# The weight differences of a seven-product block, made by GpSimd and not by VectorE

## The chip, the cores and the metric

The kernel runs on one core of a Trainium2 chip. The metric is the device time of one launch in microseconds (us). The kernel before takes 1770.96 us, the median of 3 runs (1770.84 to 1770.96).

## The reference

The reference is a chain of two transformer blocks over 512 tokens of width 1024, in fp32. The first block has windowed and block-sparse attention, the second consists of two layers with other mixers. What matters here are the three MLPs (`m0` in the first block, `m1` and `m2` in the second):

```python
y = jnp.square(jax.nn.relu(h @ w_in)) @ w_out     # w_in 1024x4096, w_out 4096x1024
x = x + y                                          # gated in m0
```

Everything else (norms, projections, attention, scans, convolution) is as before in both kernels and is not touched by the change.

## The kernel before, in words

**Precision.** Every fp32 weight of 128x1024 ("a chunk") is split in two parts before TensorE uses it. ScalarE copies the chunk, rounded, to `WH` (line 1262, `hi`), and VectorE writes the remainder, chunk minus `WH`, to `WL` (line 1852, `lo`, which counts the semaphore `w_lo`). Each product then takes three matmuls: lines 529 to 531 in `three`, and lines 855 to 857 in `product`. `WH` and `WL` have three slots (`NHL`), so `hi` of chunk n waits until TensorE is done with chunk n-3, and TensorE starts on chunk n after it has worked through n-2 and n-1.

**MLP blocks.** Each MLP is worked in four blocks of 1024 hidden features. Ten of the twelve are in the list `FAST`: (m0, 1), (m0, 2), and all four of m1 and of m2. Such a block first runs eight chunks of `w_in` (one 128x512 result each, evicted by ScalarE at line 1468 as relu and at 1470 as square; VectorE then makes differences of quarters of the hidden activations at lines 2161 to 2177 and remainders at line 2150). Then it multiplies by its 1024x1024 part of `w_out` in the way of Winograd and Strassen: seven products of quarters in place of eight (`PRODUCTS`, in the order `ORDER`). Each product has two weight chunks, c = 0 and c = 1, so a block has fourteen of them, called here half 0 to half 13: B11 (halves 0 and 1), B21 (2, 3), T2 (4, 5), T1 (6, 7), T3 (8, 9), B22 (10, 11), T4 (12, 13).

**The weight differences.** The T's are not loaded but made, by eight instructions a block (`t_add`, lines 2087 to 2106), each a subtraction of two 128x1024 fp32 tiles in SBUF: T1 = B12 - B11, T2 = B22 - T1, T3 = T2 - B11, T4 = B21 - T2, for c = 0 and c = 1. They are done in place: in `BP` (four tiles of `ARENA`) and in `TX` (one is `CSB`, the other is the last slot of `RAW`). Each waits for its loads (`park0` to `park5`) or for earlier differences (`tadd`). T3 c also waits until half c has its remainder, since it overwrites B11, and T4 c until half 4+c has its remainder, since it overwrites T2. Their readers are `hi` and `lo` of halves 4 to 9, 12 and 13. SP, which issues all weight loads, waits on `tadd` where a B21 tile in `RAW` is to be overwritten.

**Order on VectorE.** `fast_block` writes the order out: T1 of c = 0 behind input chunk 2, T1 (c = 1) and T2 (c = 0) behind chunk 4, T2 (c = 1) behind chunk 6, T3 behind steps 1 and 3 of the loop over the halves, T4 behind steps 5 and 7. Step s of that loop (1 to 13) first does the `lo` of half s+2, so that its last two steps are for chunks of what follows; the `lo` of halves 0 to 2 stand between the input chunks 5 to 7. In between, `y_read` adds finished products from PSUM (lines 2112 and 2116).

**GpSimd** has nothing to do in these blocks. Its program (line 2683 on) is 35 DMA issues and a few memsets. It waits from 309 to 702 us for the end of m0, and from 705 to 1227 us for the end of m1.

Of the kernel before, what the change touches and what calls it, by code (L numbers as in the profile page):

```python
# [13 lines left out]
ALU = mybir.AluOpType  # L14
# [29 lines left out]
FAST = (("m0", 1), ("m0", 2), ("m1", 0), ("m1", 1), ("m1", 2), ("m1", 3), ("m2", 0), ("m2", 1), ("m2", 2), ("m2", 3))  # L44
# [118 lines left out]
FB = {f: n for n, f in enumerate(FAST)}  # L163
# [29 lines left out]
def count(tag, i):  # L193

    return 32 * TAGS.index(tag) + i + 1


def count_lo(tag, i):

    return count(tag, i) + 8 * sum(f < (tag, i // 8) for f in FAST)  # L200
# [19 lines left out]
def split_of(tag, blk, p, c):  # L220

    return NO[tag + "p", 14 * blk + 2 * p + c]
# [67 lines left out]
def build(nc, W, X, CV, PAR, CON, OH, BAND, LNG, LNB, SGB, SGW, RB, OUT):  # L290
    scr = nc.dram_tensor("bias_scratch", (16, 640), F32)

    with ExitStack() as ctx:
# [3 lines left out]
        sem = Sems(lambda name: ctx.enter_context(nc.semaphore(name)))  # L297
# [18 lines left out]
        BP = [ARENA[:, 12288 + 1024 * n:13312 + 1024 * n] for n in range(4)]  # L316
        TX = [CSB[:], RAW[:, NRAW - 1, :]]
# [11 lines left out]
        def r32(ap):  # L329
            return ap.bitcast(F32)  # L330
# [70 lines left out]
        T2, acol, emc, cs8 = ar.take(S), ar.take(16), ar.take(16), ar.take(2, 32)  # L401
# [1442 lines left out]
        def vector(e):  # L1844
# [239 lines left out]
                cf, cm = COLS["final"][0], COLS["mix0"][0]  # L2084
                e.tensor_tensor(gs[:, 0:8], par[:, cf:cf + 8], par[:, cm:cm + 8], ALU.mult)

            def t_add(tag, blk, name, c):
                at = FB[tag, blk]
                b11, b12 = BP[c], BP[2 + c]
                if name == "T1":  # L2090
                    e.wait_ge(sem[f"park{c}"], 32 + 16 * (at + 1))
                    e.wait_ge(sem[f"park{2 + c}"], 32 + 16 * (at + 1))
                    e.tensor_tensor(b12, b12, b11, ALU.subtract).then_inc(sem["tadd"])
                elif name == "T2":
                    e.wait_ge(sem[f"park{4 + c}"], 32 + 16 * (at + 1))
                    e.wait_ge(sem["tadd"], 8 * at + 1 + c)
                    e.tensor_tensor(TX[c], TX[c], b12, ALU.subtract).then_inc(sem["tadd"])
                elif name == "T3":
                    e.wait_ge(sem["tadd"], 8 * at + 3 + c)
                    e.wait_ge(sem["w_lo"], split_of(tag, blk, 0, c) + 1)  # L2100
                    e.tensor_tensor(b11, TX[c], b11, ALU.subtract).then_inc(sem["tadd"])
                else:
                    e.wait_ge(sem["tadd"], 8 * at + 5 + c)
                    e.wait_ge(sem["w_lo"], split_of(tag, blk, 2, c) + 1)
                    b21 = raw((tag + "b", 10 * blk + 6 + c))[0]
                    e.tensor_tensor(TX[c], b21, TX[c], ALU.subtract).then_inc(sem["tadd"])

            def y_add(tag, row, col, tt, b, done):

                z, y = part_of(tag, row, col, tt), blocks(ps(b), 4)  # L2110
# [31 lines left out]
            def fast_block(tag, blk, norm):  # L2142
                at, lows = FB[tag, blk], count_lo(tag, 8 * blk) - 1
                adds = (tag, blk - 1) in FAST or tag == "m2"
                x0, x1, x2, x3 = [TMP[:, n, :] for n in range(4)]
                a11, a21, a12, a22 = x0[:, 0:256], x0[:, 256:512], x1[:, 0:256], x1[:, 256:512]

                def h_lo(name, k, m, src):
                    e.wait_ge(sem["mlp_hi"], lows + 4 * k + m)
                    e.tensor_tensor(combo(name, False, k), src, r32(combo(name, True, k)),  # L2150
                                    ALU.subtract).then_inc(sem["mlp_lo"])

                for c in range(8):
                    i, k, did = 8 * blk + c, c // 2, 16 * at + 4 * (c // 2)
                    if c or (tag, blk - 1) in FAST:
                        lo()
                    e.wait_ge(sem["mlp_sq"], count(tag, i))
                    if c % 2 == 0:
                        if blk or k:
                            e.wait_ge(sem["mlp_lo"], lows + 4 * k - 1)  # L2160
                        e.tensor_tensor(x2[:, 0:256], a11, a21, ALU.subtract).then_inc(sem["hs"])
                        h_lo("A11", k, 1, a11)
                        if c == 2:
                            t_add(tag, blk, "T1", 0)
                        elif c == 4:
                            t_add(tag, blk, "T1", 1)
                            t_add(tag, blk, "T2", 0)
                        elif c == 6:
                            t_add(tag, blk, "T2", 1)
                    else:  # L2170
                        e.tensor_tensor(x2[:, 256:512], a21, a22, ALU.add).then_inc(sem["hs"])
                        e.wait_ge(sem["hs"], did + 2)
                        if blk or k:
                            e.wait_ge(sem["mlp_lo"], lows + 4 * k)
                        e.tensor_tensor(x3[:, 0:256], x2[:, 256:512], a11, ALU.subtract).then_inc(sem["hs"])
                        e.wait_ge(sem["hs"], did + 3)
                        e.tensor_tensor(x3[:, 256:512], a12, x3[:, 0:256], ALU.subtract).then_inc(sem["hs"])
                        h_lo("A12A22", k, 2, x1)
                        if c == 7:
                            lo()  # L2180
                        h_lo("S31", k, 3, x2)
                        h_lo("S24", k, 4, x3)
                    if blk == 0 and c == 1:
                        token_mean(tag, norm)
                turned = (tag, blk) in TURNED
                for s in range(1, 14):
                    if turned and s in (10, 12):
                        y_read(tag, blk, ORDER[s // 2 - 1])
                        lo()
                        quarter_sum(tag, s // 2 - 4)  # L2190
                        continue
                    lo()
                    if turned and s == 9:
                        quarter_sum(tag, 0)
                    if s in (1, 3):
                        t_add(tag, blk, "T3", s // 2)
                    elif s in (5, 7):
                        t_add(tag, blk, "T4", s // 2 - 2)
                    elif s == 4 and (tag, blk + 1) not in FAST:
                        kept_read(tag, blk)  # L2200
                    elif s % 2 == 0 and s != 4 and (adds or s > 8):
                        y_read(tag, blk, ORDER[s // 2 - 1])
                    if blk == 0 and s == 4 and (tag, 3) not in FAST:
                        e.wait_ge(sem["sqrt"], NORM[norm] + 1)
                        e.reciprocal(SQ[:], SQ[:]).then_inc(sem["rb"])
                if turned:
                    late_rest(tag, 0)
                    late_rest(tag, 1)
                    y_read(tag, blk, 5)
                    late_rest(tag, 2)  # L2210
                    late_rest(tag, 3)
                    quarter_sum(tag, 3)
                    for at in range(4, 8):
                        late_rest(tag, at)
                    lo()
                    for at in range(1, 8):
                        e.wait_ge(sem["sq"], 8 * 4 + at + 1)
                        e.wait_ge(sem["ssq"], SSQ[4] + at - 1)
                        e.tensor_tensor(SQ[:], SQ[:], TMP[:, at % 4, :], ALU.add).then_inc(sem["ssq"])
                elif adds:  # L2220
                    y_read(tag, blk, 5)
# [459 lines left out]


        def gpsimd(e):
            e.memset(orow, 1.0).then_inc(sem["cs"])
            e.wait_ge(sem["g1"], 7)
            e.dma_start(con[:, NCON0:], CON[:, NCON0:]).then_inc(sem["d_con2"], 16)
# [14 lines left out]
            for n in range(8):  # L2701
                e.wait_ge(sem["mrg"], 3 * n + 1)
                e.dma_start(XT[:, n, :], X[:, S * n:S * n + S]).then_inc(sem[f"d_r{n % 4}"], 16)
            e.wait_ge(sem["mrg"], 24)
            e.wait_ge(sem["ss"], 4)
            e.dma_start(LG, LNG).then_inc(sem["d_ev"], 16)
            e.dma_start(LB, LNB).then_inc(sem["d_ev"], 16)
# [3 lines left out]
            for i in range(4):  # L2711
                last = MOFF[i] + 128 * i + 127
                e.memset(TAKE[:, :, last:last + 1], 0.0).then_inc(sem["zc"])
            e.wait_ge(sem["yx"], 8 * FTAGS.index("m1") + 8)
            e.memset(CT[:, 0, 0:3], 0.0).then_inc(sem["pad"])
            e.memset(CT[:, 1, 0:3], 0.0).then_inc(sem["pad"])
            e.memset(VO[:, :, 0:1], 1.0).then_inc(sem["pad"])

        block = ctx.enter_context(nc.Block())
        block.sync(sync)  # L2720
        block.scalar(scalar)
        block.vector(vector)
        block.gpsimd(gpsimd)
        block.tensor(tensor)

# [121 lines left out]
```

## Time and profile before

| | |
|---|---|
| median of 3 runs | 1770.96 us |
| the profiled execution, its own time | 1770.37 us |
| its span, first to last instruction | 1768.6 us |
| TensorE (PE) busy | 1747.5 us, 99% |
| VectorE (DVE) busy | 1184.5 us, 67% |
| ScalarE (ACT) busy | 886.2 us, 50% |
| GpSimd (POOL) busy | 19.5 us, 1% |
| granted TensorE clock | 1.00 of full speed in every slice |

The busy time of an engine is the time in which one of its instructions runs. A row of a timeline gives the start, the duration, the engine, the line, the operation and its tiles, and in brackets how long the engine had been idle and what ended this.

### The profile page before, as it was taken

The page shows a single profiled execution, that of the slowest core. Times are in us where ns is not written, and L with a number is a line of the kernel's source. Part 1 is how long each engine was busy: PE and PEld are TensorE (multiplying, and loading weights), DVE is VectorE, ACT ScalarE, POOL GpSimd, SP SyncE. Part 2 cuts the span into 40 slices and gives each one's busy share as a digit, 9 for nine tenths or more (in the row PEclk, how much of TensorE's full clock was granted, in tenths as well). Part 3 has the DMA queues.
Part 4 walks back from the last instruction along what each step waited for, and adds up shares of the span by engine and source line. Part 5 has one row for each costly group of instructions (what it writes and reads, how often), then busy time and mean ns, then how long its engine had stood idle before and what let it go on. Part 6 is the DMA issues. An engine that isn't in the chain of part 4 may idle for free.

```text
span 1768.6 us, 21446 instructions
## 1 busy us (share of the span) xinstructions
PE 1747.5 (99%) x8232; PEld 1434.1 (81%) x8232; DVE 1184.5 (67%) x1751; ACT 886.2 (50%) x1373; POOL 19.5 (1%) x47
## 2 busy tenths in 40 slices
PE   6999999999999999999999999999999999999999
PEld 4787788888888888888888888887888888888887
DVE  8487636674667656678566577678846557676767
ACT  4455532452546334367455546454656445454453
POOL 0100000000000000000000000000000000000000
PEclk9999999999999999999999999999999999999999
DMA  8366544234241323312333241412221241424332
GB/s 338 123 194 203 170 161 145 70 109 166 72 155 60 98 89 127 105 47 72 134 105 131 84 155 60 167 48 96 95 96 49 72 167 46 169 92 138 115 110 60
DMA packets 60855, 207.30 MB, mean 117 GB/s; under 512 B 6721, under 2 KB 11073, under 8 KB 60754
## 3 DMA queue, kind: packets, MB, share of 16 engines
q1 hardware_dynamic: 58080, 198.21, 32.4%
q0 software_dynamic: 2384, 7.51, 1.5%
q8 instruction: 66, 1.08, 0.2%
q14 instruction: 35, 0.29, 0.0%
q10 hardware_dynamic: 290, 0.22, 0.0%
HBM read 203.77 MB, written 2.14 MB: 116 GB/s over the span
## 4 chain that ended last, share of the span: by engine, by line
PE 98%; DVE 1%; ACT 0%; issue 0%; DMA 0%; DVEq 0%; ACTq 0%
PE ps L529 21%; PE ps L531 21%; PE ps L530 21%; PE ps L856 7%; PE ps L855 7%; PE ps L857 7%; PE ps L565 2%; PE ps L567 2%; PE ps L566 2%; PE ps L1130 1%; PE ps L664 1%; PE ps L1016 1%; PE ps L1061 1%; PE ps L745 1%; PE ps L719 0%; PE ps L1047 0%
## 5 line engine op out<-in xcount | busy, mean ns | idle before, releaser
L529 PE MATMUL ps<-R0h,WH 128*128 128x512 f32 x1248 | 491.9, 394 | 4.0 <-DVE R0l L1909 3.5
L531 PE MATMUL ps<-R0h,WL 128*128 128x512 f32 x1248 | 486.6, 390 | 0.0
L530 PE MATMUL ps<-R0l,WH 128*128 128x512 f32 x1248 | 486.4, 390 | 0.0
L1852 DVE TENSOR_TENSOR WL<-RAW,WH 128x1024 fp32r<-128x1024 f32 x278 | 339.3, 1222 | 160.0 <-ACT WH L1262 156.6
L1262 ACT ACTIVATE WH<-RAW 128x1024 fp32r<-128x1024 f32 x278 | 293.1, 1055 | 200.8 <-PE ps L857 100.4
L529 PEld LDWEIGHTS ps<-R0h,WH 128*128 128x128 f32 x1248 | 234.7, 188 | 56.2 <-DVE R0l L1909 4.1
L531 PEld LDWEIGHTS ps<-R0h,WL 128*128 128x128 f32 x1248 | 234.6, 188 | 49.3
L530 PEld LDWEIGHTS ps<-R0l,WH 128*128 128x128 f32 x1248 | 234.9, 188 | 47.5 <-issue 0.2
L1468 ACT ACTIVATE TMP<-ps 128x512 f32<-128x512 f32 x80 | 47.8, 597 | 184.8 <-PE ps L531 184.8
L529 PE MATMUL ps<-R1h,WH 128*128 128x512 f32 x344 | 134.6, 391 | 0.0
L531 PE MATMUL ps<-R1h,WL 128*128 128x512 f32 x344 | 133.9, 389 | 0.0
L530 PE MATMUL ps<-R1l,WH 128*128 128x512 f32 x344 | 133.8, 389 | 0.0
L855 PE MATMUL ps<-WH,R1h 128*128 128x512 f32 x320 | 124.7, 390 | 0.0
L857 PE MATMUL ps<-WH,R1l 128*128 128x512 f32 x320 | 124.5, 389 | 0.0
L856 PE MATMUL ps<-WL,R1h 128*128 128x512 f32 x320 | 124.5, 389 | 0.0
L1262 ACT ACTIVATE WH<-ARENA 128x1024 fp32r<-128x1024 f32 x60 | 63.5, 1058 | 65.6 <-PE ps L857 65.6
L856 PE MATMUL ps<-WL,HX 128*128 128x512 f32 x240 | 94.5, 394 | 0.0
L855 PE MATMUL ps<-WH,HX 128*128 128x512 f32 x240 | 94.2, 392 | 0.0
L857 PE MATMUL ps<-WH,HX 128*128 128x512 f32 x240 | 93.2, 388 | 0.0
L1852 DVE TENSOR_TENSOR WL<-ARENA,WH 128x1024 fp32r<-128x1024 f32 x60 | 73.3, 1221 | 19.3 <-ACT WH L1262 19.3
L529 PEld LDWEIGHTS ps<-R1h,WH 128*128 128x128 f32 x344 | 64.6, 188 | 13.9 <-issue 0.6
L530 PEld LDWEIGHTS ps<-R1l,WH 128*128 128x128 f32 x344 | 64.6, 188 | 13.5 <-issue 0.2
(349 smaller groups left out, 2394.9 us busy)
## 6 DMA issues: line engine op xcount, KB each, us to landing
RAW<-in_W SPq DMA_DIRECT2D x308, 512.0 KB, 3.3
ARENA<-in_W SPq DMA_DIRECT2D x52, 512.0 KB, 6.1
CSB<-in_W SPq DMA_DIRECT2D x10, 512.0 KB, 4.3
XT<-in_X SPq DMA_DIRECT2D x4, 512.0 KB, 7.8
ARENA<-bias_scratch POOLq DMA_DIRECT2D x8, 256.0 KB, 4.4
XT<-in_X POOLq DMA_DIRECT2D x8, 256.0 KB, 3.8
out_x<-XT SPq DMA_DIRECT2D x8, 256.0 KB, 2.4
ARENA<-bias_scratch POOLq DMA_DIRECT2D x8, 128.0 KB, 3.8
```

The costliest lines, as they stand in the source:

```text
L529: e.matmul(ps(b), wh, hi, start=first, stop=False)
L530: e.matmul(ps(b), wh, lo, start=False, stop=False)
L531: return e.matmul(ps(b), wl, hi, start=False, stop=last)
L565: e.matmul(ps(b), h1, wh, start=(k == 0), stop=False)
L566: e.matmul(ps(b), h1, wl, start=False, stop=False)
L567: t = e.matmul(ps(b), l1, wh, start=False, stop=last)
L855: e.matmul(ps(b), h1, wh, start=opens and k == 0, stop=False, skip_group_check=chain)
L856: e.matmul(ps(b), h1, wl, start=False, stop=False, skip_group_check=chain)
L857: t = e.matmul(ps(b), l1, wh, start=False, stop=ends and k == 3, skip_group_check=chain)
L1262: e.activation(slot(n)[0], src, ACT.Copy).then_inc(sem["w_hi"])
L1468: e.activation(x, ps(in_bank(tag, blk, c)), ACT.Relu).then_inc(sem["mlp_rr"])
L1852: e.tensor_tensor(wl, src, r32(wh), ALU.subtract).then_inc(sem["w_lo"])
```

## The change

The eight differences of each of the ten blocks leave VectorE's program, and GpSimd does them, with the same operands, the same waits and the same counts of the semaphore `tadd`. GpSimd takes them block by block, in the order T1 0, T1 1, T2 0, T2 1, T3 0, T3 1, T4 0, T4 1. Those of m0 stand ahead of GpSimd's wait for the end of m0, those of m1 ahead of its wait for the end of m1, those of m2 at the end of its program.

```diff
@@ vector, fast_block, input chunks
                         h_lo("A11", k, 1, a11)
-                        if c == 2:
-                            t_add(tag, blk, "T1", 0)
-                        elif c == 4:
-                            t_add(tag, blk, "T1", 1)
-                            t_add(tag, blk, "T2", 0)
-                        elif c == 6:
-                            t_add(tag, blk, "T2", 1)
@@ vector, fast_block, halves
-                    if s in (1, 3):
-                        t_add(tag, blk, "T3", s // 2)
-                    elif s in (5, 7):
-                        t_add(tag, blk, "T4", s // 2 - 2)
-                    elif s == 4 and (tag, blk + 1) not in FAST:
+                    if s == 4 and (tag, blk + 1) not in FAST:
                         kept_read(tag, blk)
@@ gpsimd (t_add itself moves here unchanged)
+            def t_adds(tag):
+
+                for blk in range(4):
+                    if (tag, blk) in FAST:
+                        for name in ("T1", "T2", "T3", "T4"):
+                            t_add(tag, blk, name, 0)
+                            t_add(tag, blk, name, 1)
+
...
             e.wait_ge(sem["mrg"], 24)
+            t_adds("m0")
             e.wait_ge(sem["ss"], 4)
...
+            t_adds("m1")
             e.wait_ge(sem["yx"], 8 * FTAGS.index("m1") + 8)
...
             e.memset(VO[:, :, 0:1], 1.0).then_inc(sem["pad"])
+            t_adds("m2")
```

## Rows read from the trace of the kernel before

**Rows 1.** Page, part 1: busy time, share of the span, instructions.

```profile
PE 1747.5 (99%) x8232; PEld 1434.1 (81%) x8232; DVE 1184.5 (67%) x1751; ACT 886.2 (50%) x1373; POOL 19.5 (1%) x47
```

**Rows 2.** Waits of TensorE: who waited for whom, total us, times, longest.

```profile
PE ps L577 <- DVE ARENA L1919: 9.1, 1, 9.1
...
PE ps L880 <- DVE ARENA L2116: 0.9, 1, 0.9
...
PE ps L529 <- DVE R0l L2236: 0.5, 1, 0.5
```

**Rows 3.** Groups of instructions on VectorE: count, busy us, mean ns, idle before.

```profile
L2093 DVE TENSOR_TENSOR ARENA<-ARENA 128x1024 f32<-128x1024 f32 x20 | 24.4, 1218 | 0.0
```

**Rows 4.** Groups of instructions on GpSimd, by shape.

```profile
L2717 POOL MEMSET ARENA<- 128x16 f32 x1 | 0.1, 128 | 0.0
...
L2715 POOL MEMSET ARENA<- 128x3 f32 x1 | 0.1, 100 | 522.1 <-DVE XT L2230 522.1
```

**Rows 5.** Timeline of GpSimd: its only instructions between 309 and 702 us.

```profile
701.99 0.54 POOL L2706 DMA_DIRECT2D CSB<-in_LNG  x1 [393.18 <-PE ps L577]
```

**Rows 6.** Timeline of VectorE in block (m0, 1), 454 to 505 us.

```profile
454.08 1.22 DVE L1852 TENSOR_TENSOR WL<-RAW,WH 128x1024 fp32r<-128x1024 f32 x1
...
475.84 1.22 DVE L1852 TENSOR_TENSOR WL<-ARENA,WH 128x1024 fp32r<-128x1024 f32 x1
478.22 0.43 DVE L2161 TENSOR_TENSOR TMP<-TMP 128x256 f32<-128x256 f32 x1 [1.16 <-ACT TMP L1470]
...
480.14 1.22 DVE L1852 TENSOR_TENSOR WL<-ARENA,WH 128x1024 fp32r<-128x1024 f32 x1
483.66 0.43 DVE L2171 TENSOR_TENSOR TMP<-TMP 128x256 f32<-128x256 f32 x1 [2.29 <-ACT TMP L1470]
...
485.52 1.22 DVE L1852 TENSOR_TENSOR WL<-RAW,WH 128x1024 fp32r<-128x1024 f32 x1
...
489.00 1.22 DVE L2101 TENSOR_TENSOR ARENA<-CSB,ARENA 128x1024 f32<-128x1024 f32 x1
...
503.80 1.22 DVE L2106 TENSOR_TENSOR RAW<-RAW 128x1024 f32<-128x1024 f32 x1
```

**Rows 7.** Timeline of ScalarE in the same block, 460 to 513 us.

```profile
460.60 0.60 ACT L1468 ACTIVATE TMP<-ps 128x512 f32<-128x512 f32 x1 [2.77 <-PE ps L531]
...
478.54 1.04 ACT L1262 ACTIVATE WH<-ARENA 128x1024 fp32r<-128x1024 f32 x1
...
498.85 1.06 ACT L1262 ACTIVATE WH<-ARENA 128x1024 fp32r<-128x1024 f32 x1 [1.69 <-PE ps L857]
...
512.48 1.06 ACT L1262 ACTIVATE WH<-RAW 128x1024 fp32r<-128x1024 f32 x1 [1.69 <-PE ps L857]
```

**Rows 8.** Timeline of TensorE: the first matmuls of halves 1 and 2.

```profile
484.91 0.39 PE L855 MATMUL ps<-WH,HX 128*128 128x512 f32 x1
...
487.66 0.39 PE L855 MATMUL ps<-WH,R1h 128*128 128x512 f32 x1
```

**Rows 9.** Timelines of VectorE, ScalarE and TensorE in block (m2, 1).

```profile
1568.84 1.22 DVE L1852 TENSOR_TENSOR WL<-RAW,WH 128x1024 fp32r<-128x1024 f32 x1
...
1571.61 1.06 ACT L1262 ACTIVATE WH<-RAW 128x1024 fp32r<-128x1024 f32 x1 [1.66 <-PE ps L857]
1574.33 1.07 ACT L1262 ACTIVATE WH<-ARENA 128x1024 fp32r<-128x1024 f32 x1 [1.66 <-PE ps L857]
...
1579.57 0.39 PE L855 MATMUL ps<-WH,R1h 128*128 128x512 f32 x1
```

**Rows 10.** Loads of the next block's quarters: SP's issues, landing time, VectorE then.

```profile
501.20 3.99 SPq L508 DMA_DIRECT2D ARENA<-in_W  x4
...
ARENA<-in_W SPq DMA_DIRECT2D x2, 512.0 KB, 5.5
...
510.82 1.22 DVE L1852 TENSOR_TENSOR WL<-CSB,WH 128x1024 fp32r<-128x1024 f32 x1 [1.49 <-ACT WH L1262]
...
513.57 1.23 DVE L1852 TENSOR_TENSOR WL<-RAW,WH 128x1024 fp32r<-128x1024 f32 x1 [0.32 <-ACT WH L1262]
```

More of the change, by code:

```diff
@@ L2085, in norm2 @@
                 e.tensor_tensor(gs[:, 0:8], par[:, cf:cf + 8], par[:, cm:cm + 8], ALU.mult)
[L2087 to L2106, printed above, removed]
             def y_add(tag, row, col, tt, b, done):
@@ L2683, in gpsimd, with t_add @@
         def gpsimd(e):
+            def t_add(tag, blk, name, c):
+                at = FB[tag, blk]
+                b11, b12 = BP[c], BP[2 + c]
+                if name == "T1":
+                    e.wait_ge(sem[f"park{c}"], 32 + 16 * (at + 1))
+                    e.wait_ge(sem[f"park{2 + c}"], 32 + 16 * (at + 1))
+                    e.tensor_tensor(b12, b12, b11, ALU.subtract).then_inc(sem["tadd"])
+                elif name == "T2":
+                    e.wait_ge(sem[f"park{4 + c}"], 32 + 16 * (at + 1))
+                    e.wait_ge(sem["tadd"], 8 * at + 1 + c)
+                    e.tensor_tensor(TX[c], TX[c], b12, ALU.subtract).then_inc(sem["tadd"])
+                elif name == "T3":
+                    e.wait_ge(sem["tadd"], 8 * at + 3 + c)
+                    e.wait_ge(sem["w_lo"], split_of(tag, blk, 0, c) + 1)
+                    e.tensor_tensor(b11, TX[c], b11, ALU.subtract).then_inc(sem["tadd"])
+                else:
+                    e.wait_ge(sem["tadd"], 8 * at + 5 + c)
+                    e.wait_ge(sem["w_lo"], split_of(tag, blk, 2, c) + 1)
+                    b21 = raw((tag + "b", 10 * blk + 6 + c))[0]
+                    e.tensor_tensor(TX[c], b21, TX[c], ALU.subtract).then_inc(sem["tadd"])
+            def t_adds(tag):
[4 more added lines that the diff above has]
+                            t_add(tag, blk, name, 1)
             e.memset(orow, 1.0).then_inc(sem["cs"])
```

## The prediction

> **What bounds the kernel now.** I read the busy shares first: TensorE is busy for 1747.5 of 1768.6 us, VectorE for 67%, GpSimd for 1% [rows 1]. So any gain has to come out of TensorE's 21 idle microseconds. The waits of TensorE say where they are: 9.1 us of them are one wait at the very start, for a sum of squares, and only two of TensorE's waits lie in stages that this change touches, 0.9 and 0.5 us in block (m1, 3) [rows 2]. Then I read the timelines of the three engines in one block, for one question: how long before TensorE needs it is each `lo` finished? For input chunks the cover is wide. The `lo` at 454.08 ends at 455.30, and its chunk begins only behind the one that ScalarE evicts at 460.60: 5.2 us ahead [rows 6, 7]. At the change to the products it is thin: the `lo` of half 2 ends at 486.74 and TensorE's first matmul on half 2 starts at 487.66, 0.9 us ahead [rows 6, 8]. Between halves 1 and 2 lie 2.75 us, which is the pace of the whole product stage [rows 8].
>
> **What goes.** 80 subtractions of 1.22 us [rows 3], where the other three lines have the same duration, 97.4 us of VectorE. None is waited for by TensorE, so removing them gives at most the two waits above, 1.4 us. I count no gain: the 0.9 us wait is for a product sum behind evictions and not behind a difference.
>
> **What comes.** 80 instructions on GpSimd of a duration g that this trace doesn't show. GpSimd's nearest rows are memsets, which write one stream: 128x3 in 100 ns and 128x16 in 128 ns [rows 4]. That is 28/13 = 2.15 ns a column, or 2.2 us for 1024 columns and 2.3 us with the fixed part. A subtraction has two streams to read and one to write. If each costs as much as that one, g is 6.7 us, the upper bound. The lower bound is VectorE's 1.22 us. I take 2.3 us, the row of the engine itself. The Trainium skill (GPSIMD Engine Reference, section Elementwise — side-by-side cycle accounting) gives 4497 ns for such an instruction on 2048 columns, which makes 2.25 us for 1024 as an estimate; no row here shows it, and the sum by it would be the same.
>
> **Are the differences in time, if nothing disturbs them?** T3 of c = 0 may start when half 0 has its remainder, at 475.84 + 1.22 = 477.06, and ScalarE reads it at 498.85. T4 of c = 1 is read at 512.48 [rows 6, 7]. VectorE made them at 489.00 and at 503.80, later than GpSimd will. Four GpSimd instructions in a row from 477.06 have to end by 512.48: g could be 8.8 us, above my upper bound. T1 and T2 have more room, since GpSimd can start on them when their loads land and not only behind input chunk 2. Of the waits that GpSimd gets, nothing stands behind them that is needed early: its next instruction behind the m0 ones is issued at 701.99 [rows 5], and the m1 ones stand ahead of memsets at 1227 us [rows 4]. The wait of SP on T4 ends earlier than now. All this costs nothing.
>
> **What can cost: VectorE held up.** Both engines read SBUF, and nearly all of VectorE's instructions here read two tiles from it. The trace has no GpSimd compute beside VectorE, so the cost of one running beside the other has to be bounded: from nothing (they don't disturb each other) to VectorE standing still for all of g. The Trainium skill (SBUF — State Buffer, section Who interferes with whom) speaks for the second: a VectorE instruction with two SBUF inputs and a GpSimd instruction that reads SBUF exclude each other, the later one fully blocks. I work the second case out in three places, with g left open.
>
> Place 1, the change to the products, in all ten blocks. T3 0 runs from 477.06 to 477.06 + g. The pair at 478.22 waits for it and takes 0.79 us; then comes the `lo` of half 1 (its `hi` is done at 478.54 + 1.04), which ends at 477.06 + g + 0.79 + 1.22 = 479.07 + g. That releases T3 1, which holds VectorE until 479.07 + 2g. The chain of activation differences that wants to start at 483.66 is late by 2g - 4.59, and the `lo` of half 2 behind it has 0.92 us to spare: TensorE stalls by 2g - 5.51 [rows 6 to 8]. With g = 2.3 that is below zero. The stall begins at g = 2.75 us.
>
> Place 2, T4, in all ten blocks, with the times of (m2, 1). With T3 gone, the `lo` of half 4 starts when half 3's is done and its own `hi` too, at 1570.0, and ends at 1571.2. T4 0 holds VectorE until 1571.2 + g, the `lo` of half 5 ends at 1572.4 + g (its `hi` is there at 1572.67), T4 1 runs to 1572.4 + 2g, and the `lo` of half 6 ends at 1573.6 + 2g. Half 6 is started on at 1579.57 [rows 9]. Stall: 2g - 5.9, nothing at g = 2.3.
>
> Place 3, T1 of the next block, in the seven blocks that follow another of the kind. T1 0 needs the third of the four loads that SP issues from 501.20 to 505.19. I put that issue at 504.1 and the landing 5.5 us later: T1 0 runs from about 509.6 to 509.6 + g. The `lo` that now starts at 510.82 then ends at 510.8 + g, T1 1 holds until 510.8 + 2g, and the next `lo` (now 513.57) ends at 512.0 + 2g. TensorE wants it two halves after the matmuls that released its `hi`, at 512.48 - 0.26 + 5.46 = 517.7 [rows 7, 10]. Stall: 2g - 5.7, nothing at 2.3, though a landing some tenths earlier or later shifts this.
>
> **Sum.** For g = 2.3 every place has between 0.9 and 1.3 us to spare even when VectorE stands still. Against the profiled execution, 1770.37 us (span 1768.6 and 1.8 around it): gain 0 to 1.4, cost 0 to about 2 where phases are worse than reckoned. I add 0.3 us. The median of the runs is 1770.96, 0.6 above that execution; the forecast is 1771.3 us. What 0.2% is, 3.5 us, is about the least that a measurement of this kernel can tell from no change.
>
> **Rivals.**
> 1. *VectorE is held and g is above 2.75 us.* For it: a subtraction has three streams and my row has one; the skill's rule on the shared reads; the three places all have their limits close together. Against it: at 2.3 us all have room. Price: ten times (2g - 5.51), ten times (2g - 5.9) and seven times (2g - 5.7). At g = 3.0 that is 4.9 + 1 + 2.1 = 8 us, 1779; at g = 3.3 it is 10.9 + 7 + 6.3 = 24 us, 1795; at g = 4.5, 35 + 31 + 23 = 89 us, 1860; at the upper bound it would be 200 us and more. It is over 0.2% from g = 2.9. I put it at 1785 where it happens, with a long tail. Chance 0.32.
> 2. *GpSimd is the one that is held.* VectorE's instructions stand close together from 483.66 to 504, and if GpSimd gets in only where VectorE is idle, T3 0 may come after 498.85. For it: VectorE is busy for two thirds of the time. Against it: VectorE is idle for 2.3 us before 483.66 [rows 6], T3 has 21 us, and T4 as much. If one half came 3 us late in each block: 30 us, 1801. Chance 0.04.
> 3. *Faster.* VectorE at 61% in place of 67% shortens a wait that matters. Against it: only 1.4 us of TensorE's waits can shrink, less than 3.5 us, so this would be 1769.6. Chance of over 0.2%: 0.02.
> 4. *The instructions don't land on GpSimd* or run with no effect on anything: 1771, the same as the forecast; taken with it.
>
> **How the numbers follow.** No change (forecast and rival 4): 0.62. Slower by over 0.2% is rivals 1 and 2, 0.36. Faster 0.02. The forecast alone reaches from 1769.5 to 1774. Of rivals 1 and 2 I take half into the range, up to g = 3.3, which leaves out some 0.18 above and 0.01 below: 1769 to 1795. The upper bound of g would need 1980; it stays outside as a part of that 0.18.
>
> **What would show it.** VectorE's busy time falls to about 1087 us, GpSimd's rises by 80 g, to about 204 us. The groups of lines 2093 to 2106 appear on GpSimd with g. If VectorE is held, `lo` rows beside GpSimd rows last longer than 1.22 us or start later than their `hi` allows, first at the `lo` of half 1 and the row of line 2171. If rival 1 holds, TensorE gets waits on line 1852 or 2150 at lines 855 to 857, ten of a kind; with the forecast its waits stay as they are. If rival 2 holds, ScalarE's line 1262 waits for GpSimd. I am wrong if TensorE's busy share falls below 98.5%.

## The result, and the profile after

The changed kernel takes 1783.88 us, the median of 4 runs (1782.09 to 1785.28), against 1770.96 us: the ratio is 1.0073, with a 95% interval of 1.0061 to 1.0085. It is slower by some 13 us. The forecast was 1771.3 us and no change (chance 0.62); slower had 0.36, and the range (1769 to 1795) holds the time. VectorE was held up by GpSimd, as the first rival had it, but the loss comes neither from that rival's sum nor from any of its three places.

The profiled execution took 1785.28 us, its span is 14.9 us longer. First the busy times (page, part 1), which answer to [rows 1].

```profile
PE 1754.3 (98%) x8232; PEld 1437.8 (81%) x8232; DVE 1184.0 (66%) x1671; ACT 886.6 (50%) x1373; POOL 231.7 (13%) x127
```

VectorE has 80 instructions less (1751 before) and is as busy as before. The 97.4 us that went have come back as time in which VectorE's other instructions stand still, for a row's duration contains that: the mean `lo` with its chunk in `RAW` (line 1852, 278 rows) takes 1383 ns, where it took 1222.

Line numbers differ from kernel to kernel. In the changed one T1, T2, T3 and T4 are lines 2658, 2662, 2666 and 2671 (2093, 2097, 2101 and 2106 before). VectorE's differences of activations are lines 2140 to 2149 (2161 to 2177 before), their remainders line 2129 (2150), and its readings of PSUM lines 2091 and 2095 (2112 and 2116). The groups on GpSimd (count, busy us, mean ns, idle before):

```profile
L2658 POOL TENSOR_TENSOR ARENA<-ARENA 128x1024 f32<-128x1024 f32 x20 | 59.6, 2996 | 596.6 <-DMA ARENA<-in_W 596.6
L2662 POOL TENSOR_TENSOR RAW<-RAW,ARENA 128x1024 f32<-128x1024 f32 x10 | 27.8, 2775 | 7.1 <-DMA RAW<-in_W 7.1
...
L2666 POOL TENSOR_TENSOR ARENA<-CSB,ARENA 128x1024 f32<-128x1024 f32 x10 | 24.0, 2404 | 370.8 <-DVE WL L1852 370.8
```

T3 of c = 0, which starts while VectorE is idle, takes 2.40 us, where I had put 2.3. Where VectorE comes in between, as with T1 (line 2658), the mean is 3.0 us. So each engine holds the other. Where does it reach TensorE? Its waits, answering to [rows 2]:

```profile
PE ps L529 <- DVE WL L1852: 6.3, 2, 4.0
...
PE ps L577 <- DVE SQ L1883: 1.9, 1, 1.9
...
PE ps L880 <- DVE ARENA L2095: 0.9, 1, 0.9
...
PE ps L529 <- DVE R0l L2204: 0.5, 1, 0.5
```

New are 6.3 and 1.9 us, at lines 529 (chunks) and 577 (a sum of squares), none at lines 855 to 857 (the products). By window the 4.0 lies at 890 us, at the end of the stage ahead of m1, and 2.3 and 1.9 at 1441 and 1447 us, at the end of the stage ahead of m2. In these stages VectorE adds a product to `XT` (line 1896), writes the remainder of a feature (line 1892), adds its square to `SQ` (line 1883) and makes a `lo` (line 1852). Its timeline there in the kernel before:

```profile
885.84 0.75 DVE L1892 SCALAR_TENSOR_TENSOR R0l<-XT,par,R0h 128x512 fp32r<-128x512 f32 x1 [0.79 <-ACT R0h L1299]
886.51 0.69 DVE L1883 TENSOR_TENSOR SQ<-SQ,TMP 128x512 f32<-128x512 f32 x1
887.31 1.23 DVE L1852 TENSOR_TENSOR WL<-RAW,WH 128x1024 fp32r<-128x1024 f32 x1
```

In the changed kernel, the timeline of GpSimd at the first wait, and then that of VectorE:

```profile
882.72 4.85 POOL L2658 TENSOR_TENSOR ARENA<-ARENA 128x1024 f32<-128x1024 f32 x2 [178.27 <-DMA ARENA<-in_W]
887.53 2.83 POOL L2662 TENSOR_TENSOR CSB<-CSB,ARENA 128x1024 f32<-128x1024 f32 x1
890.33 2.78 POOL L2662 TENSOR_TENSOR RAW<-RAW,ARENA 128x1024 f32<-128x1024 f32 x1
```

```profile
884.21 0.69 DVE L1896 TENSOR_TENSOR XT<-ps,XT 128x512 f32<-128x512 f32 x1 [1.26 <-PE ps L531]
885.69 2.42 DVE L1892 SCALAR_TENSOR_TENSOR R0l<-XT,par,R0h 128x512 fp32r<-128x512 f32 x1 [0.79 <-ACT R0h L1299]
888.04 2.88 DVE L1883 TENSOR_TENSOR SQ<-SQ,TMP 128x512 f32<-128x512 f32 x1
890.84 3.35 DVE L1852 TENSOR_TENSOR WL<-RAW,WH 128x1024 fp32r<-128x1024 f32 x1
```

The quarters of (m1, 0) land at 882.7 us, while VectorE is still at the last features of the stage ahead. GpSimd makes T1, T1, T2, T2 without a break. The rows of 0.75, 0.69 and 1.23 us before are now 2.42, 2.88 and 3.35 us: one behind T1 1, one behind T2 0, one behind T2 1. The row of line 1896 has only one operand in SBUF, the other in PSUM. It lies in the middle of T1 and keeps its 0.69 us. That rule, by which it takes a VectorE instruction with two SBUF inputs, was in the prediction from the Trainium skill (SBUF — State Buffer, section Who interferes with whom), and the trace bears it out: the 92 readings of PSUM at line 2095 have means of 741 and 740 ns, where they had 743.

In m2 the same four instructions start 0.6 us behind the row of line 1892, at 1436.73 us, so other rows of VectorE are held:

```profile
1436.81 2.89 DVE L1883 TENSOR_TENSOR SQ<-SQ,TMP 128x512 f32<-128x512 f32 x1
1439.62 3.38 DVE L1852 TENSOR_TENSOR WL<-RAW,WH 128x1024 fp32r<-128x1024 f32 x1
...
1445.73 2.85 DVE L1883 TENSOR_TENSOR SQ<-SQ,TMP 128x512 f32<-128x512 f32 x1
```

The first two make the wait of 2.3 us, the last one (behind T2 1) that of 1.9 us.

What the late `lo` in m1 costs is seen by windows: length; busy us (and instructions) of PE, PEld, DVE, ACT and POOL; granted clock, DMA share, GB/s.

```profile
890.00:892.00 2.00, 0.29 (x2) 0.00 (x0) 2.00 (x2) 0.00 (x0) 2.00 (x2) 1.00 0.00 0
892.00:894.00 2.00, 0.00 (x0) 0.00 (x0) 2.00 (x1) 0.00 (x0) 1.11 (x1) 0.66 0.00 0
894.00:896.00 2.00, 1.75 (x4) 1.48 (x5) 1.21 (x3) 1.17 (x3) 0.00 (x0) 0.50 0.41 98
...
898.00:900.00 2.00, 2.00 (x8) 1.56 (x7) 0.27 (x1) 0.00 (x0) 0.00 (x0) 0.63 0.34 78
900.00:902.00 2.00, 2.00 (x14) 1.81 (x13) 0.00 (x0) 0.00 (x0) 0.00 (x0) 1.00 0.54 193
```

TensorE stands for 4.0 us, and comes back at half its clock (1.2 for 2.4 GHz) until about 899.5 us. So the stall is paid more than once over. ScalarE's first eviction of m1 (line 1468) is at 907.46, before at 900.89, which with a start 0.15 us earlier makes 6.7 us: 4.0 of waiting and 2.7 of half clock. The one of m2 is at 1459.20 (1444.69 before), 7.9 us more again: 4.2 of waiting and 3.7 of half clock. The clock stays at 1.00 behind the 2.3 us there, and falls to 0.50 only behind the 1.9 us, from 1449 to about 1455.8 us. Together m1 and m2 have 14.6 of the 14.9 us.

### The profile page after: what moved, and what is told of

Same layout as the page of the kernel before. It is cut to its first block, busy times and chain, and to the rows that moved or that the text cites. A ratio compares the mean times of both kernels' runs of the same rounds, so it can differ in the third digit from the quotient of the medians.

```text
span 1783.5 us, 21447 instructions
## 1 busy us (share of the span) xinstructions
PE 1754.3 (98%) x8232; PEld 1437.8 (81%) x8232; DVE 1184.0 (66%) x1671; ACT 886.6 (50%) x1373; POOL 231.7 (13%) x127
## 4 chain that ended last, share of the span: by engine, by line
PE 96%; DVE 2%; DMA 0%; issue 0%; ACT 0%; SPq 0%; DVEq 0%; ACTq 0%
PE ps L529 21%; PE ps L531 20%; PE ps L530 20%; PE ps L856 7%; PE ps L855 7%; PE ps L857 7%; PE ps L565 2%; PE ps L567 2%; PE ps L566 2%; PE ps L1130 1%; PE ps L664 1%; DVE WL L1852 1%; PE ps L1016 1%; PE ps L1061 1%; PE ps L745 1%; PE ps L719 0%
## 5 line engine op out<-in xcount | busy, mean ns | idle before, releaser
L1852 DVE TENSOR_TENSOR WL<-RAW,WH 128x1024 fp32r<-128x1024 f32 x278 | 384.0, 1383 | 168.1 <-ACT WH L1262 164.7
L2658 POOL TENSOR_TENSOR ARENA<-ARENA 128x1024 f32<-128x1024 f32 x20 | 59.6, 2996 | 596.6 <-DMA ARENA<-in_W 596.6
L1852 DVE TENSOR_TENSOR WL<-ARENA,WH 128x1024 fp32r<-128x1024 f32 x60 | 91.1, 1530 | 19.2 <-ACT WH L1262 19.0
L2143 DVE TENSOR_TENSOR TMP<-TMP 128x256 f32<-128x256 f32 x40 | 18.7, 468 | 100.5 <-ACT TMP L1470 100.5
```

The costliest lines, as they stand in the source:

```text
L1852: e.tensor_tensor(wl, src, r32(wh), ALU.subtract).then_inc(sem["w_lo"])
```

## The experiments

Each ratio is to runs of the kernel before on the same chip. Where nothing else is said, the kernel is the changed one with the edit shown.

**e1: hold T1 and T2 of the first block until it has begun.**

```diff
-                        for name in ("T1", "T2", "T3", "T4"):
-                            t_add(tag, blk, name, 0)
-                            t_add(tag, blk, name, 1)
+                        for m, (name, c) in enumerate(itertools.product(("T1", "T2", "T3", "T4"), (0, 1))):
+                            if blk == 0 and m == 0:
+                                e.wait_ge(sem["hs"], 16 * FB[tag, blk] + 1)
+                            t_add(tag, blk, name, c)
```

> GpSimd waits, ahead of T1 of the first block of m1 and of m2 (and of m0's first, which isn't one of the ten, so nothing there), until VectorE has begun that block's activation differences; everything else is as in the changed kernel. Theory A (the 13 us are lost only where T1 and T2 of (m1, 0) and (m2, 0) fall on the end of the stage ahead): 1771 us, no wait of TensorE on line 1852, granted clock 1.000. Rival B (the held VectorE costs some tenths in every one of the ten blocks): 1776 to 1782 us. Rival C (GpSimd at work makes TensorE's clock fall by itself): above 1776 us, with a clock under 1.000 in some window.

Measured: 1783.0 us, ratio 1.0068 (1.0053 to 1.0083). Theory A is wrong for this edit, and so is the size of rival B. Rival C's two signs are there, a time above 1776 us and a clock of 0.998, but not its cause: in the windows of 904 to 912 us, with GpSimd at work all the time, the clock is 1.00, and it falls only behind waits, of which TensorE now has 4.8 us for a `lo` in m1 and 2.6 us behind a later VectorE instruction in m2. (e9 below has all 80 on GpSimd and a clock of 1.000, which puts C out.) I had moved the four into another tight stretch, and the timeline of VectorE there is the plainest picture of the hold in all the runs:

```profile
903.16 2.81 DVE L1852 TENSOR_TENSOR WL<-RAW,WH 128x1024 fp32r<-128x1024 f32 x1 [0.53 <-ACT WH L1262]
905.90 2.61 DVE L2143 TENSOR_TENSOR TMP<-TMP 128x256 f32<-128x256 f32 x1
908.54 2.50 DVE L2147 TENSOR_TENSOR TMP<-TMP 128x256 f32<-128x256 f32 x1
911.08 2.47 DVE L2149 TENSOR_TENSOR TMP<-TMP 128x256 f32<-128x256 f32 x1
```

Four GpSimd instructions, and four of VectorE, each behind one of them. Three of these take 0.42 us by themselves. The two engines take turns, and a short VectorE instruction pays as much as a long one: 2.1 us on 0.42 here, 2.1 us on the `lo` of 1.23 us in the changed kernel.

**e2: the entry alone.** T1 and T2 of (m1, 0) and (m2, 0) on GpSimd, 8 instructions; VectorE does the other 72 as before.

```diff
@@ the kernel before, vector
+                        if blk == 0:
+                            pass
-                        if c == 2:
+                        elif c == 2:
@@ vector, t_add, T3 (so that the count holds with two engines adding to it)
-                    e.wait_ge(sem["tadd"], 8 * at + 3 + c)
+                    e.wait_ge(sem["tadd"], 8 * at + 4)
@@ gpsimd, ahead of the wait for the end of m1, and at the end for m2
+                e.wait_ge(sem["tadd"], 8 * FB[tag, 0])
+                for name in ("T1", "T2"):
+                    t_add(tag, 0, name, 0)
+                    t_add(tag, 0, name, 1)
```

> Only T1 and T2 of (m1, 0) and (m2, 0) are made by GpSimd, 8 instructions in place of 80; the other 72 stay on VectorE. Theory A: all of the loss, 1780 to 1786 us, from the same two places. Rival B (loss spread over the instructions): a tenth of 13 us, 1772 us.

Measured: 1783.18 us, ratio 1.0071 (1.0056 to 1.0086), with the same waits of TensorE:

```profile
PE ps L529 <- DVE WL L1852: 6.3, 2, 4.0
...
PE ps L577 <- DVE SQ L1883: 1.9, 1, 1.9
```

A tenth of the instructions carries the whole loss. Theory A holds as to the place, and a loss spread over all blocks is out.

**e3: the same eight as memsets**, which read nothing. The differences of these two blocks are left out.

```diff
+                    if blk == 0:
+                        e.memset(b12, 0.0).then_inc(sem["tadd"])
+                    else:
                         e.tensor_tensor(b12, b12, b11, ALU.subtract).then_inc(sem["tadd"])
@@ T2 in the same way: e.memset(TX[c], 0.0)
```

> In (m1, 0) and (m2, 0) the four T1 and T2 instructions are memsets of the same 128x1024 tiles, which read nothing (these two blocks multiply by zeros or by what follows from them). The rest is as in the changed kernel. Theory A1 (VectorE is held because GpSimd reads SBUF): VectorE's rows beside the memsets keep 0.75, 0.69 and 1.22 us, 1771 us. Rival A2 (any GpSimd instruction on SBUF holds VectorE): each memset holds it for its own duration; I put that at 1 to 2.3 us, so 1773 to 1784 us.

Measured: 1770.93 us, ratio 1.0002 (0.9992 to 1.0012). In GpSimd's timeline and VectorE's, the instruction of line 1892 lies across the third memset and keeps 0.75 us:

```profile
885.50 0.96 POOL L2666 MEMSET CSB<- 128x1024 f32 x1 [0.26 <-DMA CSB<-in_W]
```

```profile
885.78 0.75 DVE L1892 SCALAR_TENSOR_TENSOR R0l<-XT,par,R0h 128x512 fp32r<-128x512 f32 x1 [0.79 <-ACT R0h L1299]
886.44 0.69 DVE L1883 TENSOR_TENSOR SQ<-SQ,TMP 128x512 f32<-128x512 f32 x1
```

Writing alone holds nothing.

**e4: T3 of c = 1 three times over**, in all ten blocks, with e1's hold.

```diff
+                    if c:
+                        for n in (1, 2):
+                            e.tensor_tensor(b11, TX[c], b11, ALU.subtract).then_inc(sem["cs"])
+                            e.wait_ge(sem["cs"], 4 + 2 * at + n)
                     e.tensor_tensor(b11, TX[c], b11, ALU.subtract).then_inc(sem["tadd"])
```

> As e1, but T3 of c = 1 is made three times over (b11 = TX - b11, which returns the same difference after three), in all ten blocks: 4.9 us more of GpSimd between its wait for half 1's remainder and its end. Theory D (VectorE and GpSimd take turns, so each VectorE instruction with two SBUF inputs is held behind one GpSimd instruction): the first differences of activations from 483.5 us are held one behind each, the remainder of half 2 ends about 491.5 in place of 486.7 and TensorE needs it at 487.7: 3 to 4.5 us of stall in each block and some 2 us more from the lower clock behind it, 1771 + 10 times 5 = 1810 to 1835 us. Rival E (GpSimd is held and VectorE goes on, or the stage has more room than I reckoned): under 1776 us.

Measured: 1833.58 us, ratio 1.0355 (1.0340 to 1.0370). This puts two more instructions on my place 1. First TensorE's wait, then VectorE's timeline in (m0, 1):

```profile
PE ps L855 <- DVE WL L1852: 33.5, 10, 3.6
```

```profile
483.27 0.56 DVE L2143 TENSOR_TENSOR TMP<-TMP 128x256 f32<-128x256 f32 x1 [2.30 <-ACT TMP L1470]
483.86 2.55 DVE L2147 TENSOR_TENSOR TMP<-TMP 128x256 f32<-128x256 f32 x1
486.45 2.52 DVE L2149 TENSOR_TENSOR TMP<-TMP 128x256 f32<-128x256 f32 x1
```

Ten waits of 3.35 us, within the expected 3 to 4.5. The sum in it started from 1771 us, but its base, e1, takes 1783: the effect is 50.6 us, 5.1 a block, of which 3.35 is waiting. The rest is the clock, but not evenly: behind eight of the ten waits it reads 0.50, for 3 us to more than 5 us, and behind the two in (m1, 2) and (m1, 3), of 3.30 us each, it stays at 1.00 in every window. So the cover at the change to the products is what I had reckoned, and two instructions more use it up.

**e5: the complement of e2.** T1 and T2 of the two first blocks by VectorE in their old places, 72 by GpSimd.

```diff
@@ gpsimd, t_adds
+                            if blk or name in ("T3", "T4"):
@@ gpsimd, t_add, T3 (the count `tadd` now comes from two engines)
+                    e.wait_ge(sem["tadd"], 8 * at + (3 + c if blk else 4 + c))
@@ vector, behind h_lo("A11", ...), as in the kernel before but only for blk 0
+                        elif c == 2:
+                            t_add(tag, blk, "T1", 0)
...
```

> The complement of e2: T1 and T2 of (m1, 0) and (m2, 0) are made by VectorE in their old places, the other 72 differences by GpSimd. Theory A (what e2 lost was all there is): 1771 us, as before, no wait of TensorE on line 1852, clock 1.000. Rival F (the other 72 cost something too, which e2 hid): 1773 us or more.

Measured: 1773.73 us, ratio 1.0016 (1.0007 to 1.0025). 10 of 13 us are gone. The time is rival F's; of the 2.9 us that are left, 2.2 are a pair of waits of 1.1 us, in (m1, 0) and (m2, 0), at half 2, which the changed kernel does not have. GpSimd's timeline, then VectorE's:

```profile
932.59 3.31 POOL L2697 TENSOR_TENSOR ARENA<-CSB,ARENA 128x1024 f32<-128x1024 f32 x1 [227.54 <-DVE RAW L2098]
935.98 2.67 POOL L2697 TENSOR_TENSOR ARENA<-RAW,ARENA 128x1024 f32<-128x1024 f32 x1
```

```profile
935.94 0.43 DVE L2174 TENSOR_TENSOR TMP<-TMP 128x256 f32<-128x256 f32 x1 [2.30 <-ACT TMP L1470]
936.40 2.54 DVE L2178 TENSOR_TENSOR TMP<-TMP 128x256 f32<-128x256 f32 x1
```

Here T3 0 had to wait for T2 1 on VectorE, which is the doing of this edit. T3 1 then falls on the activation differences, place 1 once more: one instruction is held, and with 0.9 us of cover TensorE waits 1.1.

**e6: one by one.** All 80 on GpSimd; T1 0, T1 1, T2 0, T2 1 of the two first blocks behind input chunks 2 to 5 (`m` counts the eight, as in e1).

```diff
+                            if blk == 0 and 0 <= m < 4:
+                                e.wait_ge(sem["hs"], 16 * FB[tag, blk] + (5, 8, 9, 12)[m])
```

> All 80 on GpSimd; in the first block of m1 and of m2, T1 0, T1 1, T2 0 and T2 1 start one by one, behind VectorE's activation differences of input chunks 2, 3, 4 and 5, in place of all four at once. Theory D (the cost comes where several GpSimd instructions stand in a row, since each of VectorE's is then held behind one): each of the four holds one VectorE instruction for at most 2.4 us, and input chunks have 5 us of cover: 1771 us. Rival G (the first block has no room for any of them): a stall of 1 to 3 us in each, 1775 to 1780 us.

Measured: 1773.2 us, ratio 1.0013 (1.0004 to 1.0022). TensorE has no wait at the input chunks, and one of 1.0 us at half 2 in (m1, 0), so neither theory had it quite; the other 1.4 us are not placed. One instruction at a time makes no wait where chunks have 5 us of cover.

**e7: three at the entry, the fourth behind chunk 5** (e6 with `3 <= m < 4`).

> As e6, but T1 0, T1 1 and T2 0 start when their loads land, at the end of the stage ahead, and T2 1 behind chunk 5. Theory D: in m1 the row of line 1892 and that of 1883 are held as in the changed kernel, but the `lo` behind them runs in 1.22 us and ends at about 892.1, where it ended at 894.2: TensorE stalls 2 us, not 4. If the clock's fall costs as much as before, 1778 us; if a stall of 2 us leaves the clock at 1.00, 1773 to 1775 us. Rival H (the stall is one block of time that GpSimd's four take together, not a matter of which VectorE instruction stands behind which): three quarters of the loss, 1780 us.

Measured: 1780.57 us, ratio 1.0054 (1.0040 to 1.0067). In m1 theory D has it: the `lo` behind the two held rows is free. VectorE's timeline, in which these rows come 1.4 us later than in the changed kernel:

```profile
887.07 2.43 DVE L1892 SCALAR_TENSOR_TENSOR R0l<-XT,par,R0h 128x512 fp32r<-128x512 f32 x1 [0.79 <-ACT R0h L1299]
889.42 2.88 DVE L1883 TENSOR_TENSOR SQ<-SQ,TMP 128x512 f32<-128x512 f32 x1
892.22 1.21 DVE L1852 TENSOR_TENSOR WL<-RAW,WH 128x1024 fp32r<-128x1024 f32 x1
```

TensorE waits 1.8 us there and the clock stays at 1.00. In m2 the loads land later against VectorE's work, as they did in the changed kernel: T1 0 starts 0.3 us behind the instruction of line 1892, not 3.2 us ahead of it as in m1. That one goes free, and the `lo` is held after all (3.38 us). Behind a wait of 2.3 us the clock does fall:

```profile
1440.00:1443.00 3.00, 1.82 (x6) 1.49 (x7) 2.21 (x3) 1.24 (x3) 3.00 (x2) 0.85 0.28 79
1443.00:1446.00 3.00, 3.00 (x9) 2.35 (x9) 2.67 (x3) 0.96 (x2) 0.38 (x1) 0.58 0.24 96
```

TensorE has a third wait, 1.0 us at half 2 in (m1, 0), as in e6. The time is rival H's. But m1 goes by turns as forecast, and in m2 the same three hold other instructions, as turns would have it too: what decides is which VectorE instruction meets which of GpSimd's.

**e8: every difference as two instructions of 128x512.**

```diff
+            def halves(out, a, b):
+                for n in range(2):
+                    h = slice(512 * n, 512 * n + 512)
+                    t = e.tensor_tensor(out[:, h], a[:, h], b[:, h], ALU.subtract)
+                t.then_inc(sem["tadd"])
```

> As the changed kernel, but each of the 80 is issued as two instructions of 128x512. Theory D (one VectorE instruction is held behind one of GpSimd's): rows of lines 1892, 1883 and 1852 near 886 us are held for at most 1.25 us each, the `lo` ends by 892 and the stall in m1 is at most 2 us; 1773 to 1778 us. Rival I (VectorE waits until GpSimd's queue of ready work is done): no change from the changed kernel, 1783 us.

Measured: 1776.14 us, ratio 1.0032 (1.0020 to 1.0044). The same three rows of VectorE:

```profile
885.43 1.46 DVE L1892 SCALAR_TENSOR_TENSOR R0l<-XT,par,R0h 128x512 fp32r<-128x512 f32 x1 [0.79 <-ACT R0h L1299]
886.81 1.77 DVE L1883 TENSOR_TENSOR SQ<-SQ,TMP 128x512 f32<-128x512 f32 x1
888.50 2.31 DVE L1852 TENSOR_TENSOR WL<-RAW,WH 128x1024 fp32r<-128x1024 f32 x1
```

Each is held by 0.7 to 1.1 us, half of what it was, and TensorE's waits at the two entries are 2.8 us in all, not 8.2. VectorE waits for one instruction and not for GpSimd's queue: rival I is out. Some 1.7 of the other 2.5 us are clock: in m2, behind waits of only 0.2 and 0.9 us, it reads 0.50 from about 1442.3 to 1445.8 us.

**e9: T1 and T2 of the first block where VectorE is idle**, behind the last `lo` of the stage ahead.

```diff
+                            if blk == 0 and name == "T1":
+                                e.wait_ge(sem["w_lo"], NO[tag + "i", FF[2]] + 1)
```

> All 80 on GpSimd; in the first block of m1 and of m2 T1 waits until VectorE has written the last remainder of the stage ahead (about 894 us in m1). From there VectorE has nothing to do for 8 us (8.2 us idle before its first activation difference, in the kernel before), and T1, T2 take four times 2.4 = 9.6 us. Theory D: one or two of VectorE's short instructions are held once, which the input chunks' cover takes; T3 starts where it did in the changed kernel: 1771 us, no wait on line 1852, clock 1.000. Rival G (e6's residue of 1 to 2 us comes with any placement): 1773 us.

Measured: 1771.12 us, ratio 1.0004 (0.9995 to 1.0013); 80 differences on GpSimd at no cost that can be measured. GpSimd's timeline, then VectorE's:

```profile
894.93 4.74 POOL L2658 TENSOR_TENSOR ARENA<-ARENA 128x1024 f32<-128x1024 f32 x2 [189.45 <-DVE WL L1852]
...
901.99 2.39 POOL L2662 TENSOR_TENSOR RAW<-RAW,ARENA 128x1024 f32<-128x1024 f32 x1
```

```profile
893.62 1.23 DVE L1852 TENSOR_TENSOR WL<-RAW,WH 128x1024 fp32r<-128x1024 f32 x1
903.07 1.60 DVE L2140 TENSOR_TENSOR TMP<-TMP 128x256 f32<-128x256 f32 x1 [8.22 <-ACT TMP L1470]
```

Four instructions fit into 8.2 us of VectorE's idle time but for one short hold. TensorE has no wait on line 1852. This is the fastest version with all of them on GpSimd, and it is no faster than the kernel before: nobody waited for the VectorE time that it frees.

**e10: the same eight as multiplications by -1**, one tile read. The differences of these two blocks are left out here too.

```diff
+                    if blk == 0:
+                        e.tensor_scalar(b12, b12, -1.0, None, ALU.mult).then_inc(sem["tadd"])
+                    else:
                         e.tensor_tensor(b12, b12, b11, ALU.subtract).then_inc(sem["tadd"])
@@ T2 in the same way on TX[c]
```

> As e3, but the four T1 and T2 instructions of (m1, 0) and (m2, 0) are multiplications of one tile by -1 on GpSimd: one tile read, one written (these two blocks multiply by other weights than the reference's). Theory A1 (a GpSimd instruction that reads SBUF holds VectorE for all of its own duration d): rows of lines 1892, 1883 and 1852 are held by up to d, as in the changed kernel with d for 2.4 us; with d of some 1 to 1.3 us TensorE stalls by 0 to 1 us: 1771 to 1773 us. Rival A3 (it takes two read streams to hold VectorE): the rows keep 0.75, 0.69 and 1.22 us.

Measured: 1771.09 us, ratio 1.0003 (0.9994 to 1.0012). Both theories about the rows miss. GpSimd's timeline, then VectorE's:

```profile
884.05 5.61 POOL L2659 TENSOR_SCALAR ARENA<-ARENA 128x1024 f32<-128x1024 f32 x2 [178.29 <-DMA ARENA<-in_W]
```

```profile
887.02 1.45 DVE L1892 SCALAR_TENSOR_TENSOR R0l<-XT,par,R0h 128x512 fp32r<-128x512 f32 x1 [0.79 <-ACT R0h L1299]
888.39 0.68 DVE L1883 TENSOR_TENSOR SQ<-SQ,TMP 128x512 f32<-128x512 f32 x1
889.00 1.21 DVE L1852 TENSOR_TENSOR WL<-RAW,WH 128x1024 fp32r<-128x1024 f32 x1
```

A GpSimd instruction of 2.8 us holds VectorE for 0.7 us (0.9 at most in the other rows), early in its own time. Two VectorE instructions then run their usual 0.68 and 1.21 us beside the rest of it and across its end. So the full block of the later one, as the prediction has it, holds here for GpSimd's subtractions and not for this instruction. VectorE is held only for a part in which, presumably, the tile is read; no run shows that part by itself.

## Why the prediction was right and wrong

**What bounds the kernel, and no gain:** right. The waits of 0.9 and 0.5 us are unchanged. e9 shows that the freed VectorE time is worth nothing.

**g:** 2.40 us against 2.3, right in size and by luck. The row that it was scaled from does not scale: a memset of 1024 columns takes 0.96 us (e3). The mechanism of rival 1, VectorE standing still while a GpSimd subtraction runs, was right as well. e3 and e10 point to GpSimd's reading as the cause. They do not prove it, since a memset and a multiplication differ from a subtraction in more than what they read.

**Places 1 to 3:** right, in the changed kernel. The row of line 2143 (2171 before) came to 0.56 us and the `lo` of half 2 ended at 486.72 us, 0.8 us ahead of TensorE's matmul at 487.50; it was 0.9 us before, and the sum leaves 0.7 us at g = 2.4. None of the ten blocks has a wait at lines 855 to 857. That the cover is as thin as I had it is shown by e4 (3.35 us a block), e5 and e6 (1.0 to 1.1 us).

**The step that failed** is the sentence that begins "T1 and T2 have more room, since GpSimd can start on them when their loads land". I counted that as harmless in time for the differences, and then priced only the places inside the blocks and between two of them. For (m1, 0) and (m2, 0) the loads land in the stage ahead, where VectorE's features, sums and `lo` stand close and four of GpSimd's instructions come in a row. That place has no term in the sum. Worked by the same rule it would have had one: three VectorE instructions held behind T1 1, T2 0 and T2 1 put the `lo` at about 894.2 us, where TensorE needed it at 890.1. The change does not only move work to another engine. It also removes the order in VectorE's program, which had kept T1 behind input chunk 2.

**A second term was missing:** behind a stall of 4 us TensorE ran at half clock for some 5 us in m1, and for some 7 us in m2. That adds 2.7 us to 4.0, and 3.7 to 4.2. Rival 1 priced a stall at its own length.

**The range** holds the time by luck. It reaches up to 1795 us for the sake of g above 2.75 us. At g = 2.40 rival 1's price is nothing, and the cost of 0 to 2 us that is then left in the sum does not reach 1784 us.

**Rival 2** is out: T3 took 2.4 us, and TensorE has no wait in the products of any block.

**The signs.** TensorE's busy share is 1754.3 of 1783.5 us, 98.4%: below the 98.5% at which I said I would be wrong. VectorE's busy time did not fall to 1087 us, because the profile counts the held time as busy; with VectorE standing still that sign could not come. GpSimd's rose to 231.7 us and not to 204, for it is held too.

## What to carry to other kernels

When work goes from VectorE to GpSimd, price each VectorE instruction with two SBUF inputs that can meet it at up to one whole GpSimd instruction (here 2.4 us; the held rows paid 1.7 to 2.2), and look for every stretch where GpSimd's new waits let it run, not only the one where the work stood. A queue of its own starts as early as its loads allow, so give it a wait that puts it where VectorE is idle (e9), or cut it into shorter instructions, which here took the loss from 13 to 5 us (e8). Busy time of VectorE does not tell whether it was working or held: compare the duration of one row with the same row before.

## What the runs showed of the hardware

- VectorE and GpSimd take turns where VectorE's instruction has two SBUF inputs. With ready work on both, each VectorE instruction is held behind one GpSimd instruction: four rows of 2.81, 2.61, 2.50 and 2.47 us in e1, three of them 0.42 us of work. GpSimd pays too, 3.0 us for 2.40 in the mean of T1.
- The hold goes with what GpSimd reads: none beside a memset (0.96 us), 0.7 to 0.9 us beside a multiplication that reads one tile in 2.8 us, and up to 2.2 us beside a subtraction of two tiles in 2.40 us.
- GpSimd on 128x1024 fp32: memset 0.96 us, subtraction 2.40 us, multiplication by a constant 2.8 us. The memset rows of [rows 4], 2.15 ns a column, do not scale to 1024 columns.
- The granted clock cannot be told from the length of a single wait of TensorE. It fell to 0.50 behind 4.0 us and behind 1.9 us in the changed kernel, behind 2.3 us in e7, behind 0.9 us in e8, and behind eight waits of 3.3 to 3.6 us in e4. It stayed at 1.00 behind 2.3 us in the changed kernel, behind 1.8 us in e7, behind 1.1 us in e5, and behind two waits of 3.30 us in e4. So a stall can cost its own length alone, or twice that and more.
